# The down projection as one 512-column matmul for high and low data, in two passes over half the outputs

## What is computed

```python
D_FF = ((8 * D_MODEL + 767) // 768) * 256    # 2816
for l in range(DEPTH):                       # DEPTH = 2
    h = rms_norm(x, attn_norm_g[l])
    ...
    x = x + jnp.concatenate([ya, yb, yc], axis=-1) @ w_out[l]
    h = rms_norm(x, ffn_norm_g[l])
    x = x + (jax.nn.silu(h @ ffn_w_gate[l]) * (h @ ffn_w_up[l])) @ ffn_w_down[l]
```

## Time and profile before

| what | value |
|---|---|
| median of three executions | 940.64 us |
| the profiled execution, first to last instruction (its span; no other time of it is recorded) | 938.7 us |
| TensorE matmuls busy | 916.4 us, 98% |
| VectorE busy | 680.7 us, 73% |
| ScalarE busy | 555.8 us, 59% |
| mean granted clock of TensorE | 0.997 of full |
| chain that ended last | 67% TensorE, 20% VectorE, 7% ScalarE |
| first down projection | 267.90 to 327.74 us |
| second down projection | up to 641.35 us |

### The profile page before, as it was taken

The page is one execution under the profiler, slowest core; times in us unless marked ns, Lnnn a source line. Parts: engine busy times, 40 slices in busy tenths (PEclk is TensorE's granted clock), DMA queues, the critical chain, the costliest instruction groups (busy, mean ns, idle before and its releaser), DMA issues.

```text
span 938.7 us, 20423 instructions
## 1 busy us (share of the span) xinstructions
PE 916.4 (98%) x8848; PEld 869.5 (93%) x8848; DVE 680.7 (73%) x972; ACT 555.8 (59%) x851; POOL 7.6 (1%) x12
## 2 busy tenths in 40 slices
PE   8899999999999999999999999999999999999996
PEld 7788799999999999878999999999989899989896
DVE  6899667866664589976777666448799679588675
ACT  6873566654443588355754544338587667585665
POOL 0010000000000001000000000000000000000000
PEclk9999999999999999999999999999999999999998
DMA  8342115665554544211466655554544335444231
GB/s 324 151 174 95 48 56 188 214 261 183 201 201 180 180 163 151 98 64 46 140 251 232 250 192 182 204 197 135 179 136 138 132 135 180 147 168 157 93 135 67
DMA packets 24169, 150.94 MB, mean 161 GB/s; under 512 B 2960, under 2 KB 3472, under 8 KB 7056
## 3 DMA queue, kind: packets, MB, share of 16 engines
q1 hardware_dynamic: 24080, 149.64, 44.7%
HBM read 147.26 MB, written 1.05 MB: 158 GB/s over the span
## 4 chain that ended last, share of the span: by engine, by line
PE 67%; DVE 20%; ACT 7%; issue 3%; SPq 1%; DMA 1%; DVEq 0%; ACTq 0%
PE bank L1914 9%; PE bank L1912 8%; PE bank L1913 8%; DVE w_lo L277 6%; PE bank L2145 4%; PE bank L1936 3%; PE bank L1934 3%; PE bank L1935 3%; PE bank L2146 3%; PE bank L2147 3%; ACT w_hi L271 2%; PE bank L1075 1%; PE bank L2177 1%; PE bank L589 1%; PE bank L1165 1%
## 5 line engine op out<-in xcount | busy, mean ns | idle before, releaser
L277 DVE TENSOR_TENSOR w_lo<-w_raw,w_hi 128x1024 fp32r<-128x1024 f32 x256 | 306.0, 1224 | 106.2 <-ACT w_hi L271 105.5
L271 ACT ACTIVATE w_hi<-w_raw 128x1024 fp32r<-128x1024 f32 x256 | 259.4, 1054 | 206.3 <-PE bank L1914 104.9
L1912 PE MATMUL bank<-act_hi,w_hi 128*128 128x256 f32 x704 | 194.5, 276 | 0.0
L1913 PE MATMUL bank<-act_lo,w_hi 128*128 128x256 f32 x704 | 194.3, 276 | 0.0
L1914 PE MATMUL bank<-act_hi,w_lo 128*128 128x256 f32 x704 | 194.3, 276 | 0.0
L1912 PEld LDWEIGHTS bank<-act_hi,w_hi 128*128 128x128 f32 x704 | 132.2, 188 | 0.1
L1913 PEld LDWEIGHTS bank<-act_lo,w_hi 128*128 128x128 f32 x704 | 132.2, 188 | 0.0
L1914 PEld LDWEIGHTS bank<-act_hi,w_lo 128*128 128x128 f32 x704 | 132.2, 188 | 0.0
L2145 PE MATMUL bank<-act_hi,w_hi 128*128 128x256 f32 x352 | 100.2, 285 | 0.3
L2147 PE MATMUL bank<-act_hi,w_lo 128*128 128x256 f32 x352 | 97.7, 278 | 0.0
L2146 PE MATMUL bank<-act_lo,w_hi 128*128 128x256 f32 x352 | 97.7, 278 | 0.0
(11 more groups left out here) (367 smaller groups left out, 1982.1 us busy)
## 6 DMA issues: line engine op xcount, KB each, us to landing
w_raw<-in_w_ffn SPq DMA_DIRECT2D x66, 1024.0 KB, 4.8
w_raw<-in_w_mix SPq DMA_DIRECT2D x62, 1024.0 KB, 4.9
small_w<-in_small SPq DMA_DIRECT2D x2, 1280.0 KB, 7.6
w_raw<-in_w_mix SPq DMA_DIRECT2D x8, 256.0 KB, 6.3
x_res<-in_x_channels SPq DMA_DIRECT2D x4, 256.0 KB, 6.1
probs<-in_w_mix SPq DMA_DIRECT2D x2, 512.0 KB, 7.5
probsT<-in_w_mix SPq DMA_DIRECT2D x1, 1024.0 KB, 10.1
mem<-in_mem_channels SPq DMA_DIRECT2D x1, 1024.0 KB, 7.2
```

What stands on the lines that cost most here:

```text
L271: self.nc.scalar.activation(hi, self.piece(self.raw_slot(g), p), ACT.Copy).then_inc(self.hi_ready, 1)
L277: self.nc.vector.tensor_tensor(lo, self.piece(self.raw_slot(g), p), hi.bitcast(fp32), ALU.subtract).then_inc(self.lo_ready, 1)
L1912: TE.matmul(o, hi[:, w], HI[:, k, :], start=(k == 0 and x == 0), stop=False)
L1913: TE.matmul(o, hi[:, w], LO[:, k, :], start=False, stop=False)
```

## The change

The low parts of the data lie behind the high parts in one array (`act`, `gated_split`), so that one matmul can stream both: 256 columns of high data and 256 of low data against the same high weights, into the two halves of one bank. A second matmul of 256 columns adds low weights by high data to the second half. A tile so has two matmuls and two weight loads instead of three and three, and a pair of outputs takes two banks instead of one. All eight outputs would then need all eight banks, so the down projection is made in two passes: outputs 0 to 3 in banks 4 to 7 over all k, then outputs 4 to 7 in banks 0 to 3. The weights are laid out in that order (`DOWN_TILES`), with the same number of chunks. The halves of a bank are added where x is updated: two additions for each pair (`x_add_halves`). The pairs 0 and 1 of x are updated, converted and squared in the course of the second pass. Gate and up chunks rotate over eight banks instead of four.

The core of the diff:

```diff
+DOWN_TILES = [(k, o) for h in (0, 4) for k, o in
+              [(k, h + x) for k in range(FK - 4) for x in range(4)] + [(k, h + x) for x in range(4) for k in range(FK - 4, FK)]]
...
     def wait_out(self, eng, p):
 
-        if p % 2:
+        if self.down and p in (0, 3):
+            eng.wait_ge(self.K.st.chunk_used, self.chunk - (0 if p else 6))
+        elif self.down:
+            eng.wait_ge(self.K.sem("out_done"), 2 * (self.n - 1) + p)
+        elif p % 2:
...
+    def x_add_halves(self, dve, ch, p, halves):
+        x = self.K.X[:, 2 * p:2 * p + 2, :]
+        self.wait_out(dve, p)
+        ch(self.nc.vector.tensor_tensor(x, x, halves[:, :, 0, :], ALU.add))
+        self.nc.vector.tensor_tensor(x, x, halves[:, :, 1, :], ALU.add).then_inc(self.K.sem("x_new"), 1)
...
     def bank_of(i):
 
-        return banks[i - 2] if i in (4, 5) else banks[4 + (i if i < 4 else i - 6) % 4]
+        return banks[i - 2] if i in (4, 5) else banks[(4 + (i if i < 4 else i - 6)) % 8]
...
+    def down_bank(o):
+
+        return banks[(o + 4) % 8]
+
     def down_part(pe, i, p):
 
         hi, lo = st.slot(i)
-        if i < LAST:
-            steps = [(2 * (i - DOWN) + p // 2, 4 * (p % 2) + x) for x in range(4)]
-        else:
-            steps = [(FK - 4 + x, 4 * (i - LAST) + p) for x in range(4)]
         if p % 2 == 0:
             st.arrived(pe, i, p // 2)
-        if i == LAST and p == 0:
-            pe.wait_ge(*at("gated_lo", NB))
-        elif i < LAST and p == 0:
-            pe.wait_ge(*at("gated_lo", i - DOWN + 1))
-        for x, (k, o) in enumerate(steps):
-            w = slice((4 * p + x) * P, (4 * p + x + 1) * P)
-            out = banks[o // 2][:, (o % 2) * T:(o % 2 + 1) * T]
-            TE.matmul(out, hi[:, w], GHI[:, k, :], start=(k == 0 and o % 2 == 0), stop=False)
-            TE.matmul(out, hi[:, w], GLO[:, k, :], start=False, stop=False)
-            last = TE.matmul(out, lo[:, w], GHI[:, k, :], start=False, stop=(k == FK - 1 and o % 2 == 1))
+        if i == DOWN and p == 0:
+            pe.wait_ge(*at("gate_used", NB - 2))
+            pe.wait_ge(*at("up_used", NB - 2))
+        for x in range(4 * p, 4 * p + 4):
+            k, o = DOWN_TILES[16 * (i - DOWN) + x]
+            if o == 0 and k % 2 == 0:
+                pe.wait_ge(*at("gated_lo", k // 2 + 1))
+            w, bank = slice(x * P, (x + 1) * P), down_bank(o)
+            TE.matmul(two(bank), hi[:, w], GHL[:, :, k, :], start=(k == 0), stop=False)
+            last = TE.matmul(bank[:, T:2 * T], lo[:, w], GHI[:, k, :], start=False, stop=(k == FK - 1))
         if p == 3:
             last.then_inc(st.chunk_used, 1)
-        elif i >= LAST and p == 1:
+        elif p == 1 and i in (DOWN + 5, N - 1):
             last.then_inc(sem("out_done"), 1)
...
+            elif i == DOWN + 5:
+                x_add(dve, ch, 0)
+            elif i == DOWN + 6:
+                x_add(dve, ch, 1)
+            elif i == DOWN + 7:
+                after.lo(dve, 0)
+                after.lo(dve, 1)
+            elif i == DOWN + 8:
+                after.square_sum(dve, 1)
```

More of the change, by code:

```diff
@@ L189, in __init__ @@
         raw = K.sb("w_raw", [P, 2, CHUNK], top=True)
-        hi, lo = (K.sb(f"w_{x}", [P, 2, CHUNK], f32r, top=True) for x in ("hi", "lo"))
+        self.w = K.sb("w_split", [P, 2, 2, CHUNK], f32r, top=True)
+        lo, hi = self.w[:, 0, :, :], self.w[:, 1, :, :]
         self.raw = [raw[:, i, :] for i in range(2)]
@@ L302, in __init__ @@
         self.X = self.sb("x_res", [P, KT, T])
[L303 to L304 removed]
+        self.HL = self.sb("act", [P, 2, KT, T], f32r)
+        self.HI, self.LO = self.HL[:, 0, :, :], self.HL[:, 1, :, :]
         self.PRMS = self.sb("prm", [P, WIDTH["prm"] + N_PRMS], top=True)
@@ L346, with __init__ @@
 class Norm:
-    def __init__(self, K, n, chunk, gain):
-        self.K, self.nc, self.n, self.chunk, self.gain = K, K.nc, n, chunk, gain
+    def __init__(self, K, n, chunk, gain, down=False):
+        self.K, self.nc, self.n, self.chunk, self.gain, self.down = K, K.nc, n, chunk, gain, down
     def wait_out(self, eng, p):
-        if p % 2:
+        if self.down and p in (0, 3):
[3 more added lines that the diff above has]
+        elif p % 2:
             eng.wait_ge(self.K.st.chunk_used, self.chunk - 1 + p // 2)
@@ L432, in __init__ @@
     def __init__(self, K, n, chunk, gain, g1, SQ2, R1):
-        super().__init__(K, n, chunk, gain)
+        super().__init__(K, n, chunk, gain, down=True)
         self.g1, self.SQ2, self.R1 = g1, SQ2, R1
@@ L1903, in proj_part @@
         if p == 0 and i >= 6:
-            pe.wait_ge(*at("up_used" if i % 2 else "gate_used", (i - (6 if i < 10 else 4)) // 2 + 1))
+            before = i - 6 if i < 10 else i - 8
+            pe.wait_ge(*at("up_used" if i % 2 else "gate_used", max(before // 2, 0) + 1))
         if p % 2 == 0:
@@ L1990, in _ @@
     def _(pe):
-        for p in range(4):
-            proj_part(pe, 0, p)
-        for i in range(1, DOWN):
+        for i in range(DOWN):
             for p in range(4):
@@ L2022, in _ @@
                 gated_hi(act, i // 2 - 1)
-        after.hi(act, 0)
-        after.squares(act, 0)
-        if layer == 1:
-            after.scaled_squares(act, 0)
+            elif i == DOWN + 6:
+                after.hi(act, 0)
+                after.hi(act, 1)
+            elif i == DOWN + 7:
+                after.squares(act, 0)
+                after.squares(act, 1)
+            elif i == DOWN + 8 and layer == 1:
+                after.scaled_squares(act, 0)
+                after.scaled_squares(act, 1)
         st.split_hi(act, N, 0)
-        after.hi(act, 1)
         st.split_hi(act, N, 1)
         after.hi(act, 2)
-        after.squares(act, 1)
         after.squares(act, 2)
+        st.split_hi(act, N + 1, 0)
         after.hi(act, 3)
         after.squares(act, 3)
-        st.split_hi(act, N + 1, 0)
-        if layer == 1:
-            after.scaled_squares(act, 1)
     @block.vector
@@ L2066, in _ @@
                 gated_lo(dve, i // 2 - 1)
-        after.x_add(dve, 0, banks[0])
-        after.lo(dve, 0)
-        after.x_add(dve, 1, banks[1])
+            elif i == DOWN + 5:
+                x_add(dve, ch, 0)
+            elif i == DOWN + 6:
+                x_add(dve, ch, 1)
+            elif i == DOWN + 7:
+                after.lo(dve, 0)
+                after.lo(dve, 1)
+            elif i == DOWN + 8:
+                after.square_sum(dve, 1)
         st.split_lo(dve, N, 0)
-        after.lo(dve, 1)
-        after.x_add(dve, 2, banks[2])
+        x_add(dve, ch, 2)
         st.split_lo(dve, N, 1)
         after.lo(dve, 2)
-        after.x_add(dve, 3, banks[3])
-        after.square_sum(dve, 1)
+        x_add(dve, ch, 3)
+        st.split_lo(dve, N + 1, 0)
         after.lo(dve, 3)
@@ L2784, in turn @@
                                                     self.scaled[:, k * T + t * P:k * T + (t + 1) * P], self.K.cst("ident"))
-        last.then_inc(self.K.sem("out_turned"), 1)
+        last.then_inc(*self.K.up("turned"))
         pe.wait_ge(self.K.sem("square_sum"), 4 * self.n + 4)
@@ L2849, in program @@
                 if layer == 0:
-                    after = Norm(K, 2, N_MIX1 + N_FFN, K.prm(N_PRM + Q_G, KT))
+                    after = Norm(K, 2, N_MIX1 + N_FFN, K.prm(N_PRM + Q_G, KT), down=True)
                     with ExitStack() as c1:
@@ L2928, in layout @@
     parts = [x[..., 256 * b:256 * (b + 1)] for b in range(FK // 2) for x in (gate, up)]
-    parts += [down[:, :, 2 * q:2 * q + 2, :] for q in range(FK // 2 - 2)] + column_chunks(down[:, :, -4:])
+    blocks = [down[:, :, k, o * P:(o + 1) * P] for k, o in DOWN_TILES]
+    parts += [np.concatenate(blocks[16 * q:16 * q + 16], 2) for q in range(FK // 2)]
     io["w_ffn"] = flat_chunks(parts)
```

19 lines of the change are left out of this document (11 added, 8 removed).

## The result

The changed kernel takes 943.82 us (median of 7 runs, 943.05 to 944.39), the kernel before 940.64 (7 runs, 939.58 to 942.03). The ratio is 1.0036 with an interval of 1.0027 to 1.0046: slower by 0.36%, about 3.2 us. The forecast was 937.7, with 935.9 to 940.6 as its range and "slower" at 0.07.

The account below looks back on a forecast made before the run. TensorE's matmul stream was taken to bound the down projections. Stream -4.05 us, exits +0.9 and +0.2, sum -2.95: from 940.64 to 937.7 us, range 935.9 to 940.6.

Parts of the forecast that it names:

- What bounds the kernel: In the two down projections, 119.7 us together, only TensorE's matmul stream counts; VectorE and ScalarE have room.
- The step that failed: Down projection: a 512-column matmul hides the next weight load, so a tile takes 328.5 ns, not 340; saves 4.05 us.
- the 6.7 ns: Down projection: excess of the measured 113.3 ns step over the 106.7 ns that 256 columns take at 2.4 GHz.
- the load 0.60 + 0.14: Chances of the two cases with load-paced down steps: late exit, 937.7 us (0.60), and free exit, 936.0 us (0.14).
- the last rival: Down projection: alternating widths bring the stream's slower spacing, 354 ns a tile, +4.9 us; chance 0.06.
- its 946.6: Whole-kernel time in us if the down stream takes its slower spacing: +4.9 for the stream and +1.1 for the exit.
- the third case of the forecast: Down projection: surcharge goes with columns, 512 cost 226.7 ns, tile stays 340; only the exit remains, 941.7 us; chance 0.13.
- The exit: Behind each down projection: late sum of squares stalls TensorE, costing +0.9 us after layer 0 and +0.2 after layer 1.
- The walk: Exit chain followed by durations: fold ends at t0 + 6.2, row sums start at t0 + 6.3, t0 being next stage's start.
- the 0.1 us taken for its going: Exit after layer 1: 0.1 us taken back because one split fewer stands on VectorE before the scaled squares.
- act_lo comes in time: Next stage's chunk 0: last two channel tiles wanted at 4.08 and 4.76 us, ready about 4.0 and 4.4; no stall.
- One reading: Down projection's exit: the time 317.12 was taken as the end of the last but one down chunk.

Follow-up runs that it names:

- experiment 10: Changed kernel with 256-column matmuls only, one half bank and one addition per pair, and the whole exit order of the kernel before: 940.51 us, ratio 1.0002.
- experiment 5: Changed kernel with a single 512-column matmul at the head of each down projection, all others 256 columns: 944.28 us, ratio 1.0048.
- experiment 4: Kernel before with down chunks 2 to 10 replaced by probe matmuls of various widths, not computing the projection: 984.5 us, one run, whole time meaningless.
- experiment 1: Changed kernel with the 512-column matmul split into two of 256 again; passes, layouts and exit order stay: 940.08 us, ratio 0.9993.
- 2: Changed kernel with 256-column matmuls only, all three products in one half bank and one addition per pair: 939.19 us, ratio 0.9986.
- 6: Changed kernel with one 512-column matmul per down projection, plus a plain fp32 transpose ahead of the third down chunk: 945.48 us, one run.
- 8: Changed kernel plus one fp32 transpose on TensorE behind each down projection: 944.50 us, ratio 1.0056.
- 9: Changed kernel with 256-column matmuls, one addition per pair, and the next stage's second-chunk split back behind the squares: 938.93 us, ratio 0.9988.

## Why the prediction was wrong, point by point

**What bounds the kernel** was read rightly: in the down projections only the matmul stream counts. There is no idle time before or after, the eight banks are worth nothing (experiment 10), and the whole loss lies in the step between matmuls.

**The step that failed** is this one: "If they come from the weight load that has to finish behind each matmul, a 512-column matmul hides its successor's load and pays almost nothing." Of the 4.05 us that it promised none came. The load is not where the 6.7 ns come from: with 64 weight columns instead of 128 the steps stay (119.0 beside 117.7, 232.7 beside 233.3), while their loads are 54 ns shorter. (That bf16 steps by 109.1 proves less, since its loads are shorter too, 98 ns.) The surcharge goes with the columns of the fp32r data: 0.451 ns each for 0.417 at the slower level, and at the better one 226 ns for the first wide matmul of each projection, which is twice 113.3 (226.7). Both rows that spoke for the load were read over the fence of a data type: the earlier trace rows are plain fp32, of which 256 columns step by 215 ns where fp32r has 113, and the single-column matmuls of the earlier trace rows show only that a load fits into 0.11 us, not that it sets the step of a matmul that takes as long. The text named fp32 as its weak point and still gave the load 0.60 + 0.14.

**What came on top** is the mechanism of the last rival, "the alternation of widths puts the stream into its slower spacing", with a chance of 0.06: it gave 354 ns for a tile, and 353.2 were measured. Its name is not quite right. No alternation is needed: here one 512-column matmul does it, and 526 short ones behind it pay (experiment 5). Nor is a wide matmul needed: the kernel before changes level behind two late steps at 39 us, and in experiment 4 the level after wide matmuls is the better one. The evidence held against it, mixed widths in the earlier trace rows, was fp32 again, while the row for it, 0.12 in the earlier trace rows, was fp32r, and the 94 steps of 117.8 ns that follow it in that trace had not been followed up. It is worth 4.7 us. What it put beside that, 1.1 us for the exit, was too much, and so its 946.6 lay above the time measured.

So even a stream that stayed on its better level would, as an estimate, have won nothing: 226.7 + 113.3 is 340, the third case of the forecast ("the 6.7 ns go with the columns"). No run held a stream of wide matmuls on that level.

**The exit** was to cost 0.9 and 0.2 us. With 340 ns tiles (experiment 1) it cost 0.6 after layer 0 and gave 0.6 back after layer 1. The walk was right in its order and late in its end: row sums at t0 + 5.97 for 6.3, a stall of 0.37 for 0.8. What it missed is the other side of the same move. After layer 1 the work on the first half, its squares and scaled squares, had stood behind the last chunk, and the 0.1 us taken for its going was too little; with single additions the second exit gives 1.1 us, about 0.5 by the row sums and the rest by the second, scaled sum. Which of the moved pieces brings it no run separates. The second additions cost 0.9 us in the new order (experiments 1 and 2, whose intervals overlap) and in the old one about 3 (948.05 - 4.7 of stream - 940.5 of experiment 10 = 2.9; by the traces 1.7 and 1.6, with 0.4 of chunk 0's slower steps in it). That act_lo comes in time held: no idle time stands before the last two channel tiles. One reading was off by a chunk: 317.12 is the end of the ninth of the eleven down chunks (267.90 + 9 x 5.44 = 316.86), not of the last but one, and nothing in the sum hung on it.

**The sum**, by the traces: +4.7 for the stream, +0.3 and -1.0 for the exits, and -0.6 in the rest of the program, among it -1.2 for the DMA that VectorE did not wait for and +0.4 for the stretch near the end that ran on the slower level; no step of the change explains either. That is 3.4 for 3.2 by the medians. The exits are 0.6 us better together than in experiment 1, although chunk 0 ends 0.2 later. In part a longer chunk 0 takes up the stall: the row sums are 0.22 us late behind it here and 0.53 there. In part it is the level: behind the row sums the stream steps by 113.3 here after both layers (337.1 to 347.4 and 652.4 to 657.4) and by 117.8 in experiment 1 (334.2 to 345.2 and 648.5 to 653.9), 0.4 and 0.2 us. How much each is worth was not separated. The forecast's 0.9 for the first exit was a term of the right sign and too large; its 0.2 for the second had the wrong sign.

**What stays open.** What puts a stream on one level or the other, and what brings it back, is not settled. In the changed kernel it comes back behind the row sums (117.7 before 335.4, 113.3 from 337.1), but the same row sums after layer 0 take the kernel before from 113.3 to 117.8, and leave experiments 5, 6 and 8 on 117.8. Late steps can change it in a stream of 256 columns alone, and two attempts with a transpose, in the stream (6) and behind it (8), did not bring it back. Why fp32r pays 4% (113.3 for 109.1) or 8% (117.7) more than bf16 is not shown either.

**The best versions** are experiments 2 and 9, with 256-column matmuls, two passes, one addition a pair and the first pairs handled early: 939.19 and 938.93 us, 0.12 to 0.14% below the kernel before.

## What to carry to other kernels

Price a matmul by the step between starts in rows of its own data type; a row in another type, or a duration, says nothing of it. Where a new width enters a stream, look also at the steps of the unchanged instructions behind it: here one 512-column fp32r matmul made 526 others dearer by 4%. Look in the trace of before as well for stretches in which the same instruction has another step: it showed the slower level, for 94 steps on end, before anything was changed. And since the level outside the changed place differs from one trace to the next by 0.4 to 0.6 us in a stretch, compare a stage with itself, and not the ends of two traces. What paid in this change was the part that looked like bookkeeping, converting and squaring finished outputs while the stream still works on the second half.

## What the runs showed that I had not expected

At a granted clock of 1.00, an fp32r stream steps by 113.3 or by 117.7 ns for 256 columns and stays where it is while nothing interrupts it, through hundreds of instructions and through chunk boundaries; behind a late step, a row sum or a wide matmul it can be on either. At 512 columns it steps by 226 (the first, and every other one when two of 256 follow each) or 231 to 236. Between 256 and 512 columns the price is 0.451 ns a column, with no step at a width that would pay. bf16 steps by 109.1 and 215.8. Weights with half the columns are not cheaper on the slower level. A 128-column bf16 load, 98 ns long, and a 256-column bf16 matmul fit into 109.1 together.
